# Block products for the last quarter of the MLP input of a hybrid decoder layer

## The reference, cut to what matters

```python
x = x + rms_norm(y, post_norm_mix[l])
h = rms_norm(x, pre_norm_mlp[l])
y = jnp.square(jax.nn.relu(h @ w_mlp_in[l])) @ w_mlp_out[l]
x = x + rms_norm(y, post_norm_mlp[l])
```

## Time and profile before

| | us |
|---|---|
| median of 3 runs | 748.58 (748.31 to 748.79) |
| profiled execution | 748.65 |
| its span | 747.1 |
| PE busy | 739.8 |
| DVE, ACT, POOL busy | 436.2, 389.3, 317.3 |

### The profile page before, as it was taken

One profiled execution on the slowest core, in us unless ns is written; L12 is line 12 of the kernel. 1 busy time (PEld: TensorE's weight loads), 2 busy tenths in 40 slices (PEclk: granted clock), 3 DMA queues, 4 the chain that ended last, 5 costly groups with the idle time before them and its releaser, 6 DMA issues.

```text
span 747.1 us, 11902 instructions
## 1 busy us (share of the span) xinstructions
PE 739.8 (99%) x4168; PEld 608.1 (81%) x4168; DVE 436.2 (58%) x651; ACT 389.3 (52%) x632; POOL 317.3 (42%) x296
## 2 busy tenths in 40 slices
PE   9999999999999999999999999999999999999996
PEld 7788778888887878788888988888888888888885
DVE  5896899990444545345974511221221777778795
ACT  6657842268555365635655733332332655565671
POOL 2357894535444754574526454645645000000002
PEclk9999999999999999999999999999999999999999
DMA  9336223446365577266651279789877476654752
GB/s 341 102 93 205 57 77 108 127 128 184 113 156 157 192 174 204 60 159 204 207 183 29 84 244 290 186 269 282 231 238 212 159 222 197 197 186 153 219 174 113
DMA packets 52893, 129.21 MB, mean 173 GB/s; under 512 B 6096, under 2 KB 6512, under 8 KB 50544
## 3 DMA queue, kind: packets, MB, share of 16 engines
q1 hardware_dynamic: 49120, 109.47, 44.7%
q0 software_dynamic: 3392, 18.88, 13.1%
q10 hardware_dynamic: 336, 0.28, 0.1%
HBM read 126.49 MB, written 39.86 MB: 223 GB/s over the span
## 4 chain that ended last, share of the span: by engine, by line
PE 93%; POOL 3%; ACT 2%; DVE 1%; issue 0%; POOLq 0%; ACTq 0%; DVEq 0%
PE bank L758 28%; PE bank L760 27%; PE bank L759 27%; POOL rsq L2158 2%; PE bank L1005 1%; PE bank L1028 1%; PE bank L1015 1%; POOL w_lo L2164 1%; PE bank L969 1%; PE bank L779 1%; PE bank L933 1%; PE bank L785 1%; PE bank L980 1%; PE bank L1037 1%; PE bank L788 0%; PE bank L1067 0%
## 5 line engine op out<-in xcount | busy, mean ns | idle before, releaser
L2164 POOL TENSOR_TENSOR w_lo<-raw,w_hi 128x512 fp32r<-128x512 f32 x169 | 220.0, 1311 | 238.4 <-ACT w_hi L1220 236.6
L1220 ACT ACTIVATE w_hi<-raw 128x512 fp32r<-128x512 f32 (+2 forms) x214 | 144.9, 684 | 156.3 <-PE bank L760 122.6
L758 PE MATMUL bank<-h_hi,w_hi 128*128 128x512 f32 (+1 forms) x528 | 208.5, 395 | 0.2
L759 PE MATMUL bank<-h_lo,w_hi 128*128 128x512 f32 (+1 forms) x528 | 204.2, 387 | 0.0
L760 PE MATMUL bank<-h_hi,w_lo 128*128 128x512 f32 (+1 forms) x528 | 204.1, 387 | 0.0
L758 PEld LDWEIGHTS bank<-h_hi,w_hi 128*128 128x128 f32 x528 | 99.1, 188 | 25.5 <-issue 5.1
L760 PEld LDWEIGHTS bank<-h_hi,w_lo 128*128 128x128 f32 x528 | 99.2, 188 | 20.6
L759 PEld LDWEIGHTS bank<-h_lo,w_hi 128*128 128x128 f32 x528 | 99.3, 188 | 18.7
L1629 DVE SCALAR_TENSOR_TENSOR relu_sb<-bank,rs_row 128x512 f32<-128x512 f32 x32 | 20.6, 686 | 126.0 <-PE bank L760 114.3
L2305 POOL TENSOR_SCALAR ssh<-ssy 128x1 f32<-128x1 f32 x4 | 1.0, 238 | 151.6 <-ACT junk L1600 151.6
L758 PE MATMUL bank<-w_hi,a_hi 128*128 128x512 f32 x120 | 46.8, 390 | 0.0
(11 more groups left out here) (327 smaller groups left out, 1260.8 us busy)
## 6 DMA issues: line engine op xcount, KB each, us to landing
raw<-in_w_in SPq DMA_DIRECT2D x87, 256.0 KB, 2.7
raw<-in_w_mlp_in SPq DMA_DIRECT2D x62, 256.0 KB, 5.1
t_sum<-in_w_mlp_out POOLq DMA_DIRECT2D x12, 1024.0 KB, 9.0
raw<-in_w_mlp_out SPq DMA_DIRECT2D x26, 256.0 KB, 2.7
raw<-t_sum SPq DMA_DIRECT2D x26, 256.0 KB, 2.9
v_sum<-in_w_mlp_out POOLq DMA_DIRECT2D x4, 1024.0 KB, 9.4
raw_b<-in_w_mlp_out SPq DMA_DIRECT2D x16, 256.0 KB, 2.9
raw_b<-t_sum SPq DMA_DIRECT2D x14, 256.0 KB, 2.9
```

Of the source, the lines that this page charges most:

```text
L758: pe.matmul(o, s_hi, m_hi, start=start, stop=False, skip_group_check=True)
L759: pe.matmul(o, s_hi, m_lo, start=False, stop=False, skip_group_check=True)
L1220: return a.activation(o, i_, ACT.Copy, scale=scale)
L2164: g.tensor_tensor(w_lo[:, slot, :], raw[:, slot, :], w_hi[:, slot, :].bitcast(F32), ALU.subtract).then_inc(lo_ready, 1)
```

## The change

Groups 0 to 11 of the MLP input stay as they are. The last 1024 columns (four groups, 16 units) become two **steps** of 14 units. h is split into four blocks (two halves of the features, two halves of the tokens), the weights of a step into four blocks (two halves of the features, two column blocks of 256). A step makes seven block products q1 to q7, two units each, with 256 tokens as the moving operand, so 28 units of 12 matmuls of 256 columns.

- The block sums of h are made once: DVE adds high and low part of each block (4 instructions of 128 x 1024) and takes 4 differences, ACT rounds them (4), DVE makes their low parts (4).
- The block sums of the weights are made by transfers, as for the output: four copies on SP and four accumulating ones on POOL's queue, 1 MB each, beside units 48 to 70 (`IN_SUM_AT`).
- In a step, 10 of 14 low parts are made by DVE and 4 by POOL. Loads go through a ring of 8. ACT copies product q1 out of its banks, DVE makes five more sums per block column out of banks, with 256 columns each, and two ReLUs of 512 columns out of SBUF. PE waits for these sums before q7, q3, q4 and, in the next step, q1, q6 and q5.
- The sums of `w_mlp_out` are moved: eight beside units 64 to 118, eight behind groups 1 to 11; the one of group 11 is copied there and added by POOL at unit 7 of the first step.
- x after the mixer is copied to HBM behind loads of groups 2 and 3 (four transfers of 512 KB), since its place is needed, and read back during the MLP output; the vector `post_norm_mlp` is loaded there too, no longer behind unit 116.
- The first block product of the MLP output starts after the last step's sums; the last step's ReLUs lie in DVE's queue within `one(1)`.

```diff
-U_M1 = U_OUT + 64
+G_PLAIN = 12
+F_HALF = (FF - G_PLAIN * 256) // 2
+U_S = U_OUT + 4 * G_PLAIN
+STEPS_IN = F_HALF // 256
+PER_STEP = 14
+RING = 8
+U_M1 = U_S + STEPS_IN * PER_STEP
-OUT_SUM_AT = {48: 0, 52: 1, 60: 2, 87: 3}
+OUT_SUM_AT = {55: 0, 61: 1, 70: 2, 85: 3}
-SUM_AT = {61: (0, 0), 65: (1, 0), 73: (2, 0), 74: (0, 1), 78: (1, 1), 86: (2, 1)}
+SUM_AT = {64: (0, 0), 73: (1, 0), 76: (2, 0), 79: (0, 1), 82: (1, 1), 88: (2, 1), 113: (0, 2), 118: (1, 2)}
+IN_SUM_AT = {48: (0, 0), 51: (1, 0), 58: (2, 0), 68: (3, 0)}
-SUM_IN = {2: (0, 2), 3: (0, 3), 4: (3, 0), 5: (3, 1), 7: (2, 2), 8: (2, 3), 9: (1, 2), 10: (1, 3), 12: (3, 2), 13: (3, 3)}
+SUM_IN = {1: (0, 3), 2: (3, 0), 3: (1, 3), 4: (2, 2), 5: (3, 1), 6: (2, 3), 9: (3, 2), 11: (3, 3)}
+IN_PRODUCTS = ("q1", "q6", "q5", "q2", "q7", "q3", "q4")
+LOW_POOL = (1, 3, 7, 11)
+LOW_DVE = tuple(v for v in range(PER_STEP) if v not in LOW_POOL)
...
+        def in_product(s, name):
+            if name == "q1":
+                pe.wait_ge(made_in, made("c11", s - 1, 1)) if s else pe.wait_ge(relu_done, 2 * G_PLAIN - 2)
+            elif name == "q6":
+                pe.wait_ge(made_in, made("c21", s - 1, 1)) if s else pe.wait_ge(relu_done, 2 * G_PLAIN)
...
+            for half in range(2):
+                u = U_S + PER_STEP * s + 2 * IN_PRODUCTS.index(name) + half
+                pe.wait_ge(*low_of(u))
+                for kk in range(2):
+                    for e in range(2):
+                        c = slice(kk * 256 + e * P, kk * 256 + e * P + P)
+                        x_ = three(bank[IN_BANK[name] + e][:, 0:256], w_hi[:, u % SPL, c], w_lo[:, u % SPL, c],
...
+        def split_in(u):
+            a.wait_ge(*raw_signal(u))
+            a.wait_ge(unit_done, u - 3)
+            copy(w_hi[:, u % 4, :], raw_of(u)).then_inc(hi_ready, 1)
...
+                if v_ == 10:
+                    v.wait_ge(unit_done, u)
+                    v.wait_ge(made_in, made("f", s, 1))
+                    for e in range(2):
+                        v.tensor_tensor(relu_sb[:, 2 * e + 1, 256:512], bank[2 + e][:, 0:256], f1[:, e, :], ALU.subtract).then_inc(made_in, 1)
...
+                in_low(u + LEAD)
+                if v_ in (7, 9):
+                    combine_in(G_PLAIN - 2 + 2 * s + v_ // 2 - 3)
+                if s == STEPS_IN - 1 and v_ == 10:
+                    a_low(0, 0, slice(0, 4), 1)
+                if s == STEPS_IN - 1 and v_ in (12, 13):
+                    w_low(v_ - 12, 1, v_ - 11)
```

More of the change, by code:

```diff
@@ L1494, in mlp_in @@
                     a.wait_ge(row_full, 1)
-                    mark(copy(rs_row[:], bank[7][:]), row_ready)
+                    mark(copy(rs_row, bank[7][:]), row_ready)
+                    mark(copy(rs_ext[:, 0:256], bank[7][:, 256:512]), row_ready)
                     square_group(i, 0)
[L1497 to L1502, removed]
+                if not (first and j < 3):
@@ L1503, in mlp_in @@
                     split(None, u % 4, i * 32 + 16 * loads(u), i * 8 + (u - 3))
-                if j == 3 and not first or j == 7 and not last:
+                if j == 3 and not first or j == 7:
                     square_group(i, j // 4)
+                if blocks and j in (2, 3, 4, 5):
+                    a.wait_ge(diffs_made, OUT_G + j - 1)
+                    if j == 2:
+                        a.wait_ge(copied_out, 16 * (1 + NT))
+                    b = T_ORDER[j - 2]
+                    copy(ts_hi[b][:], t_full[b][:]).then_inc(dhi_ready, 1)
@@ new lines, in split_in, with mlp_in_last @@
+        def split_in(u):
+            a.wait_ge(*raw_signal(u))
+            a.wait_ge(unit_done, u - 3)
+            copy(w_hi[:, u % 4, :], raw_of(u)).then_inc(hi_ready, 1)
+        def mlp_in_last(i):
+            for j in range(8):
+                u = U_OUT + LEAD + 8 * i + j
+                if u < U_S:
+                    split(None, u % 4, 16 * loads(u), u - 3)
+                else:
+                    split_in(u)
+                if j in (3, 7):
+                    square_group(i, j // 4)
@@ L1517, in _, with one @@
         mlp_in(0, True)
-        with a.Fori(1, 7) as i:
+        with a.Fori(1, 3) as i:
             mlp_in(i, False)
-        mlp_in(7, False, True)
-        def one(i, last=False):
+        mlp_in(3, False, True)
+        for i in range(4, G_PLAIN // 2 - 1):
+            mlp_in(i, False)
+        mlp_in_last(G_PLAIN // 2 - 1)
+        for s in range(STEPS_IN):
+            mlp_in_step(s)
+        def one(i, last=False, ends=False):
             for g in range(4):
+                if ends and g == 2:
+                    for e in range(2):
+                        square_in(STEPS_IN - 1, e)
                 a.wait_ge(part_done, i * 8 + (2 * g + 2 - 8))
@@ L1544, in _ @@
         a_split(1, 1, slice(0, 4))
-        square_group(NI - 1, 1)
         w_split(6, 2, 16)
-        with a.Fori(1, NI - 1) as i:
+        one(1, ends=True)
+        with a.Fori(2, NI - 1) as i:
             one(i)
@@ L2040, in _ @@
             relu(i, ms=(2, 3))
[L2041 to L2048, removed]
+            combine(2 * i - 1)
+        for s in range(STEPS_IN):
+            step_in(s)
+        w_low(2, 1, 3)
+        v.wait_ge(unit_done, U_M1)
+        for e in range(2):
+            c21(STEPS_IN - 1, e)
         w_low(3, 1, 4)
@@ L2053, in _ @@
         s4(0)
-        with v.Fori(1, NI - 1) as i:
+        one(1, ends=True)
+        with v.Fori(2, NI - 1) as i:
             one(i)
@@ L2264, in _ @@
             out_low(e)
+        g.wait_ge(*copied(0, 3))
+        g.dma_start(*t_add(0, 2), accum_op=ALU.add, max_dma_last_dim=8192).then_inc(t_added[0], 16)
         g.wait_ge(lo_ready, U_PLAIN + 4)
```

329 lines of the change are left out of this document (276 added, 53 removed).

## The result

The changed kernel took **750.53 us** (median of ten runs, 749.01 to 753.0); the kernel before, 748.55 us beside it (ten runs, 748.31 to 748.93). The ratio is 1.0029, with a 95% interval of 1.002 to 1.0037: slower by 2 us, where 2.2 us faster was forecast, and outside the range given. The scatter grew too, from 0.6 to 4 us, so what was added doesn't cost the same each time. The profiled execution took 750.15 us (span 748.4, against 747.1).

The account below looks back on a forecast made before the run. TensorE was taken as the bound, busy 739.8 of 747.1 us. Matmuls -3.2, unit 114 +0.7, entry +0.1 and exit +0.2 gave -2.2 us, so 746.4 us, range 745.0 to 749.4.

Parts of the forecast that it names:

- Matmuls: Last 16 MLP input units: 192 matmuls of 512 columns become 336 of 256, 43.5 to 40.3 us, gain 3.2 us.
- The larger gain: Rival: a 256-column step matmul takes exactly half of a 512-column one, gain 5.4 us, 744.2 us; chance 0.02.
- Feeding the steps: Inside the two steps: work of DVE, ACT and POOL fits in 20.2 us per step, so no PE wait.
- the rival of a late DVE: DVE needs 20.2 and 22.7 us in the steps, leaves the second 2.5 us late; 748.7 us, chance 0.20.
- Entry: Start of the steps, fourth step unit: low part ready barely in time, cost 0.1 us, range 0 to 0.5.
- Unit 114: MLP input: a sum's copy behind unit 113's load delays unit 114's load, so PE waits 0.7 us.
- Exit: End of the second step: DVE has about 0 spare before the second a_lo; PE waits 0.2 us, range 0 to 2.5.
- Loads: Weight loads in the steps and beside x's copies in groups 2 and 3 land in time; cost 0, bound about 1 us.
- other late loads: Rival: weight loads other than the one at unit 114 land late and make PE wait; chance 0.06.
- The rival that ended slower: The copy at unit 113 makes unit 114's load land after 11.2 us, PE waits 4.9 us; 750.6 us, chance 0.12.

Follow-up runs that it names:

- the version without stalls: Changed kernel with sums behind groups 1, 4, 5, 6, 8 to 11, unit 113's copy behind unit 116, last step's ReLUs and squares later: 745.74 us.
- the spread order: Changed kernel with its eight plain-group sums behind groups 1, 4, 5, 6, 8 to 11 instead of 1 to 6, 9, 11: 747.31 us.

## Why the prediction was wrong

- **Matmuls, -3.2 us: right.** 40.31 us for the 28 units, 0.1200 us a matmul, and the version without stalls gains 3.3 us of span. The larger gain (5.4) is refuted.
- **Feeding the steps, no stall: right.** DVE is busy 14.9 and 17.2 us in them, of 20.2, and PE waits for nothing; the rival of a late DVE (20.2 and 22.7) had it meet POOL every time, and that much lost time isn't there. **Entry:** 0.1 forecast, none seen.
- **Unit 114, 0.7 us: right in mechanism and size.** Six profiles with the copy there show 0.26, 1.32, 1.09, 0.68, 1.22 and 1.05 us, 0.94 in the mean, and without it none. The load of unit 114 landed 6.9 us after its issue in the changed kernel and 7.5 to 7.9 in the other five; the working had 7.0. The changed kernel's own profile has the smallest stall of the six.
- **Exit, 0.2 us (0 to 2.5): mis-sized.** 0.52 us in each profile with the ReLUs in their place. The working added 1.2 us for two ReLUs, as of 512 columns. Those out of SBUF have 768 (the text on the change says 512), and each takes 0.87 us from its start to the next:

```profile
596.03 0.95 DVE L1837 SCALAR_TENSOR_TENSOR relu_sb<-relu_sb,rs_ext 128x768 f32<-128x768 f32 x1
596.90 0.42 DVE L2216 TENSOR_TENSOR act<-act 128x256 f32<-128x256 f32 x1
```

  That is 1.74 us, 0.54 more, where the working had left about zero to spare.
- **"Loads", "Cost 0, upper bound about 1 us": this step failed.** It measured 3.2 us. The prediction compared a slack of 14.8 us with the worst landing of the kernel before, 11.2 us, and both sides were wrong. A landing does not belong to a kind of place: with 2.1 MB more and two more sums in a row the loads landed up to 13.8 us after their issue, and the same loads in the spread order in 9.4 at most. Nor is the slack a constant. The chain through the stretch (start, length) names the load behind each of the four stalls:

```profile
432.89 13.21 DMA raw<-in_w_mlp_in
...
446.92 2.55 POOL w_lo L2476 x2
449.47 0.02 issue
449.49 10.69 DMA raw<-in_w_mlp_in
...
462.31 9.26 DMA raw<-in_w_mlp_in
...
478.52 13.83 DMA raw<-in_w_mlp_in
```

  PE was late by 0.58, 0.31, 0.64 and 1.24 us, so these loads had 12.6, 10.4, 8.6 and 12.6 us, not 14.8. Two of them landed faster than 11.2 us and still stopped PE: a late load makes a late low part, that low part frees its slot late (446.92 + 2.55 = 449.47), and the next load goes out late. The sum of volumes above, kept up from group to group, would have shown a backlog of 8.7 us where the prediction saw none, from rows of the trace of before; it would not have given the 3.2, since a backlog of 7.8 cost 0.2. The chance of 0.06 for other late loads rested on the same comparison.
- **The rival that ended slower** gave 750.6 us, close to the result, by the copy at unit 113, which was to stall PE 4.9 us at unit 114. That is a coincidence: the stall there is 0.26 us in the changed kernel's profile.

## What to carry to other kernels

When a change adds transfers under a stage that already uses most of the DMA engines' time, price each kind per MB from the queue shares, sum them per group, and carry the surplus on to the next group; a landing time from a quieter stretch is no bound for it, and the slack of a load shrinks once the loads ahead of it are late. Where no bytes can be taken out of a stage, their order can be changed: the same bytes, with the light groups between the heavy ones, cost nothing here and took the scatter away. Before moving an instruction to another place in one engine's queue, look who waits for it on the others, and move that too.

## What the runs showed of the hardware beyond that

Accumulating transfers within HBM took 5.08 us of the DMA engines per MB, and the plain loads and copies beside them 2.86 (the kernel before, 411 to 540 us), so an add weighed nearly two copies. And a stall of PE costs more than the wait: the first matmul behind it is recorded at 0.50 us instead of 0.39, the second starts 0.34 us behind instead of 0.23, 0.10 or 0.11 us more at each stall looked at.
